# Sampled attention split in two: chosen blocks gathered into DRAM by SyncE, attended after the prompt's attention

## What is computed

```python
def token_mix_sample(xn, cache_cmp, cache_slc, cache_win, wkv, shift, page_table, lw):
    ...
    o_cmp, sel_idx, sel_ok = cmp_attend_select(q, compress(cmp_full, lw), q_pos, slc_full.shape[1] // L_SLC)
    o_slc = slc_attend(q, q_pos, sel_idx, sel_ok, slc_full.reshape(B, -1, L_SLC, 2, N_KV, HEAD_DIM))
    ...
    o_win = window_sample(q, q_pos, win_all, k_pos)
    nsa_out = nsa_combine(gates, o_cmp, o_slc, o_win)

def slc_attend(q, q_pos, sel_idx, sel_ok, kv_blocks):
    ...
    g = kv_blocks[bi, sel_idx, :, :, hi, :]
    s = jnp.einsum('bthgd,bthnld->bthgnl', q, g[..., 0, :]).astype(jnp.float32) * SCALE
    ...
    p = masked_softmax(s, mask[:, :, :, None], axis=(-2, -1))
    return jnp.einsum('bthgnl,bthnld->bthgd', p.astype(g.dtype), g[..., 1, :])
```

## Time and profile before

| | us |
|---|---|
| median of 3 runs | 3992.76 |
| lowest, highest | 3984.46, 3997.12 |
| profiled execution, its own time | 3984.06 |
| its span, first to last instruction | 3982.4 |
| sampled stage, first issue to last store's issue | 1640.09 to 1873.68 |
| prompt's stage, first to last issue of SyncE | 1882.21 to 2203.68 |

### The profile page before, as it was taken

How to read it: one execution, slowest core, us unless ns; L and a number is a source line. 1 busy time by engine, 2 the same in 40 slices (tenths; PEclk the granted TensorE clock), 3 DMA queues, 4 the chain that set the end, 5 groups by cost and what they waited for, 6 DMA issues and landing times. The chain is left out here.

```text
span 3982.4 us, 68983 instructions
## 1 busy us (share of the span) xinstructions
PE 3496.3 (88%) x29788; PEld 3150.0 (79%) x29788; DVE 1489.0 (37%) x1881; ACT 975.6 (24%) x1332; POOL 474.5 (12%) x525
## 2 busy tenths in 40 slices
PE   5999998669927899744799898999999999999998
PEld 5999997358826777522433798999999999999997
DVE  3222220743265767311355323333333333333334
ACT  4111110622213444100243323212212121221112
POOL 1000000444503333200000000000000000000000
PEclk8999997679968999777799999999999999999999
DMA  5343331555515442342300232333333323323332
GB/s 165 108 115 110 93 106 27 192 167 146 119 36 211 179 184 111 98 105 75 109 6 11 80 85 76 95 96 86 96 93 88 96 87 94 96 85 96 91 90 96
DMA packets 501130, 408.07 MB, mean 102 GB/s; under 512 B 142965, under 2 KB 453702, under 8 KB 496262
## 3 DMA queue, kind: packets, MB, share of 16 engines
q1 hardware_dynamic: 454982, 282.91, 25.5%
q0 software_dynamic: 14816, 113.89, 7.8%
q10 hardware_dynamic: 31104, 7.88, 0.9%
HBM read 366.16 MB, written 50.02 MB: 105 GB/s over the span
## 5 line engine op out<-in xcount | busy, mean ns | idle before, releaser
L2574 DVE TENSOR_TENSOR f_w_lo<-wo_raw,f_w_hi 128x2048 fp32r<-128x2048 f32 x132 | 302.5, 2292 | 808.4 <-ACT f_w_hi L2546 808.4
L53 PE MATMUL d_ps<-hh,f_w_hi 128*128 128x260 f32 x2816 | 567.5, 283 | 11.4 <-DVE f_w_lo L2574 11.4
L57 PE MATMUL d_ps<-hh,f_w_lo 128*128 128x260 f32 x2816 | 568.5, 284 | 0.0
L55 PE MATMUL d_ps<-hl,f_w_hi 128*128 128x260 f32 x2816 | 567.6, 283 | 0.0
L2546 ACT CAST f_w_hi<-wo_raw 128x2048 fp32r<-128x2048 f32 x132 | 252.0, 1909 | 995.1 <-DMA wo_raw<-in_w_gate 396.4
L53 PEld LDWEIGHTS d_ps<-hh,f_w_hi 128*128 128x128 f32 x2816 | 435.2, 189 | 11.8 <-DVE f_w_lo L2574 11.8
L57 PEld LDWEIGHTS d_ps<-hh,f_w_lo 128*128 128x128 f32 x2816 | 435.2, 189 | 0.0
L55 PEld LDWEIGHTS d_ps<-hl,f_w_hi 128*128 128x128 f32 x2816 | 433.8, 189 | 0.0
L53 PE MATMUL d_ps<-f_hid_hi,f_w_hi 128*128 128x260 f32 x1408 | 283.7, 283 | 1.2 <-DVE xt L2598 1.2
L57 PE MATMUL d_ps<-f_hid_hi,f_w_lo 128*128 128x260 f32 x1408 | 283.5, 283 | 0.0
L55 PE MATMUL d_ps<-f_hid_lo,f_w_hi 128*128 128x260 f32 x1408 | 282.5, 282 | 0.0
(11 more groups left out here) (431 smaller groups left out, 5941.9 us busy)
## 6 DMA issues: line engine op xcount, KB each, us to landing
p_w<-in_w_in SPq DMA_DIRECT2D x46, 1024.0 KB, 5.6
wo_raw<-in_w_gate SPq DMA_DIRECT2D x44, 1024.0 KB, 5.6
wo_raw<-in_w_up SPq DMA_DIRECT2D x44, 1024.0 KB, 5.6
wo_raw<-in_w_down SPq DMA_DIRECT2D x44, 1024.0 KB, 5.1
wo_raw<-in_w_o SPq DMA_DIRECT2D x16, 1024.0 KB, 6.0
rk_chunks<-r_outb POOLq DMA_DIRECT2D x8, 1280.0 KB, 6.2
s_cur<-rk_chunks SPq DMA_DIRECT2D x8, 1280.0 KB, 7.2
s_one_vecs<-samp_rows SPq DMA_DIRECT2D x80, 128.0 KB, 4.5
```

The costliest lines, as they stand in the source:

```text
L53: pe.matmul(out[j], w_hi, x_hi[j], start=start, stop=False)
L55: pe.matmul(out[j], w_hi, x_lo[j], start=False, stop=False)
L57: last = pe.matmul(out[j], w_lo, x_hi[j], start=False, stop=stop)
L2574: dve.tensor_tensor(w_lo[:, s, :], w_raw[:, s, :], w_hi[:, s, :].bitcast(F32), ALU.subtract).then_inc(lo_done, 1)
```

## The change

The sampled stage becomes two. The first, `stage_nsa_select`, keeps the compressed and the window branch, all of the choice of blocks, and 26 of the gathers. The second, `stage_nsa_picked`, does the attention over chosen blocks, and stands behind the prompt's stage.

- **Gathers.** Their destination is no longer `kbuf` but a new DRAM tensor, `sel_d` [8, 2, 128, 8, 256]. SyncE issues 26 in the first part, 338 in the prompt's stage behind `wo_ahead` (sequences 0, second half, to 6), and ScalarE the 52 of sequence 7 in the second part. The row of addresses is loaded again in each (`places_in`). The page halves that are always attended also go to `sel_d`, all 16 on SyncE.
- **First part.** `win` has 16 slots in memory of its own and GpSimd loads all of them without waiting. ScalarE, not VectorE, copies the turned keys. The importance product moves behind the first turn. The sum of the two branches is kept in `o_part`.
- **Second part.** SyncE loads `sel_d`, keys through three slots and values whole; 16 units, two groups, as before; `o_part` is added; SyncE stores.
- **Prompt.** The four stores move from SyncE to GpSimd, and `mo` has one slot per half instead of two.

```diff
+def gather(eng, g, adr_row, regs, b, heads):
...
+    for hh in heads:
+        for k0 in range(0, 16, 4):
+            at = (b * 4 + hh) * 16 + k0
+            eng.load(regs, adr_row[0:1, at:at + 4])
+            for n in range(4):
...
+                page = eng.snap(regs[n], min_val=0, max_val=places - 1)
+                eng.dma_start(g.sel_d[b, :, lo:lo + C, k // 2, hh * C:(hh + 1) * C].rearrange("v r d -> r v d"),
+                              cache[bass.ds(page, 1), :, :, hh, :].rearrange("a r v d -> r (a v) d")).then_inc(g.sel_kept[b], 16)
...
-                for b in range(NB):
-                    gather(sp, regs, b, 0)
-                sp.wait_ge(os_ready, 1)
...
+                gather(sp, g, adr_row, regs, 0, (0, 1))
...
-                pool.wait_ge(cmp_done, 1)
                 for n in range(2 * NB):
-                    b, kv, s = n % NB, n // NB, n % 3
-                    if 3 <= n < 3 + NB:
-                        pool.wait_ge(kturned, n - 2)
-                    elif n >= 3 + NB:
-                        pool.wait_ge(wv_done, n - 2 - NB)
...
+                for n in range(NB):
+                    act.wait_ge(kturned, n + 1)
+                    if n >= 2:
+                        act.wait_ge(kmm, n - 1)
+                    bank = 2 * (n % 2)
+                    act.copy(kT[:, n % 2, :], ps[:, bank:bank + 2, :].rearrange("p b n -> p (b n)")).then_inc(kept, 1)
...
-                for b in range(2):
-                    gather(act, regs, b, 1)
                 act.wait_ge(nmax_ready, 2)
                 act.activation(sw[:], ps[:, 4, :], ACT.Exp, bias=st[:, 2, 1:2], accum_out=st[:, 2, 2:3]).then_inc(exp_done, 1)
-                for b in range(2, 6):
-                    gather(act, regs, b, 1)
-                picked_exp(0)
...
+def stage_nsa_picked(nc, g):
...
+                def rows_in(dst, b, v, sem_):
+                    sp.dma_start(dst[:, 0:NT - 1, :], g.sel_d[b, v, :, 0:NT - 1, :]).then_inc(sem_, 16)
+                    sp.dma_start(dst[0:C + 1, NT - 1, :], g.sel_d[b, v, 0:C + 1, NT - 1, :]).then_inc(sem_, 16)
+
+                def keys_in(b):
+                    if b >= 3:
+                        sp.wait_ge(kturned, 2 * (b - 2))
+                    sp.wait_ge(g.sel_kept[b], 16 * 4 * (NS - 3))
+                    rows_in(kb[:, b % 3], b, 0, k_in[b % 3])
...
+                keys_in(0)
...
+                            sp.dma_start(qs[a * C:(a + 1) * C, h, :, :], heads[a, :, h]).then_inc(q_in, 16)
+                keys_in(1)
+                keys_in(2)
+                for b in range(NB):
+                    rows_in(vb[:, b], b, 1, v_in[b // 4])
+                    if b + 3 < NB:
+                        keys_in(b + 3)
...
+                    places_in(act, g, adr_row, adr_in)
+                gather(act, g, adr_row, regs, NB - 1, range(4))
...
                 wo_ahead(sp, g)
-                for i in range(4):
-                    sp.wait_ge(o_kept, 4 * i + 4)
-                    sp.dma_start(g.mix_t[D_R + i * 256:D_R + i * 256 + 256, 0:SEQ].rearrange("(g d) t -> d g t", d=C),
-                                 mo[half(i), i // 2, :, :]).then_inc(mix_stored, 16)
-                sp.wait_ge(mix_stored, 16 * 4)
+                regs = [sp.alloc_register(f"picked_place{n}") for n in range(4)]
+                with nc.allow_non_contiguous_dma(reason="small tables"):
+                    places_in(sp, g, adr_row, adr_in)
+                gather(sp, g, adr_row, regs, 0, (2, 3))
+                for b in range(1, NB - 1):
+                    gather(sp, g, adr_row, regs, b, range(4))
...
                 mix_ahead(pool, g)
+                for i in range(4):
+                    pool.wait_ge(o_kept, 4 * i + 4)
...
                 stage_nsa_prompt(nc, g)
+                stage_nsa_picked(nc, g)
```

More of the change, by code:

```diff
@@ L1621, in stage_nsa_sample @@
         adr_ready, adr_out, adr_in = sem("adr_ready"), sem("adr_out"), sem("adr_in")
[L1622 to L1625, removed]
+        win_loaded = [sem(f"win_loaded{n}") for n in range(2 * NB)]
@@ L1631, in stage_nsa_sample @@
-        new = g.kv_rows[SEQ:TC, 512:1024].rearrange("b (v h d) -> b v h d", v=2, h=4)
         pages = g.cache_slc.rearrange("n (t r) w -> n t r w", t=2)
[L1635 to L1656, removed]
@@ L1658, in stage_nsa_sample @@
-        ALL = 16 * 2 * (NS - 3)
+        new = g.kv_rows[SEQ:TC, 512:1024].rearrange("b (v w) -> b v w", v=2)
         with nc.Block() as block:
@@ L1671, in _ @@
                         sp.dma_start(ptb[16 * b:16 * b + 16, :], g.page_table[b:b + 1, :].to_broadcast([16, PG])).then_inc(pt_in, 16)
-                    sp.dma_start(kbuf[C:C + 1, :, NS // 2 - 1].rearrange("p b v h d -> p b (v h d)"),
-                                 g.kv_rows[SEQ:TC, 512:1024].unsqueeze(0)).then_inc(new_in, 16)
-                regs = [sp.alloc_register(f"sp_place{n}") for n in range(4)]
+                    sp.dma_start(g.sel_d[:, :, C, NS // 2 - 1, :], new).then_inc(g.sel_always, 16)
+                regs = [sp.alloc_register(f"sel_place{n}") for n in range(4)]
                 sp.wait_ge(row_in, 32)
-                always(sp, regs, 0)
+                for b in range(NB):
+                    sp.load(regs[0:2], pt_row[0:1, b, :])
+                    for n in range(2):
+                        page = sp.snap(regs[n], min_val=0, max_val=PLACES // 2 - 1)
+                        lo = C - n * C
+                        sp.dma_start(g.sel_d[b, :, lo:lo + C, NS // 2 - 2 + n, :].rearrange("v r w -> r v w"),
+                                     pages[bass.ds(page, 1), n].rearrange("a r (v w) -> r (a v) w", v=2)).then_inc(g.sel_always, 16)
                 with nc.allow_non_contiguous_dma(reason="small tables"):
@@ L1730, in turn @@
                         pe.wait_ge(kept, n - 1)
[L1731 to L1745, removed]
+                    pe.wait_ge(win_loaded[n], 48)
+                    for h in range(2):
+                        for t in range(4):
+                            last = pe.transpose(ps[:, bank + h, t * P:(t + 1) * P], win[:, n, t, h * P:(h + 1) * P], g.ident[:])
                     last.then_inc(kturned, 1)
@@ L1749, in mult @@
                     pe.wait_ge(kept, n + 1)
[L1750 to L1762, removed]
+                    for h in range(2):
+                        last = pe.matmul(ps[:, 4, :], query(n, h, 0, P), kT[:, n % 2, h * 512:(h + 1) * 512],
+                                         start=(n + h == 0), stop=(n + h == NB))
                     last.then_inc(kmm, 1)
@@ L2060, in _ @@
                 mix_ahead(pool, g)
+                for i in range(4):
+                    pool.wait_ge(o_kept, 4 * i + 4)
+                    pool.dma_start(g.mix_t[D_R + i * 256:D_R + i * 256 + 256, 0:SEQ].rearrange("(g d) t -> d g t", d=C),
+                                 mo[half(i), :, :]).then_inc(mix_stored[i % 2], 16)
+                for s in range(2):
+                    pool.wait_ge(mix_stored[s], 32)
             @block.tensor
@@ L2204, in keep_out @@
                     act.wait_ge(pv_done, first_block[2 * m + 1] + t + 1)
-                    act.copy(mo[half(i), i // 2, :, t * P:(t + 1) * P],
+                    if i >= 2 and t == 0:
+                        act.wait_ge(mix_stored[i % 2], 16)
+                    act.copy(mo[half(i), :, t * P:(t + 1) * P],
                              ps[half(i), 6 + m % 2, :].rearrange("p (q t) -> p q t", q=4)).then_inc(o_kept, 1)
@@ L2848, in build @@
     g.adr_d = nc.dram_tensor("adr_d", [P, 16], I32, kind="Internal").ap()
+    g.sel_d = nc.dram_tensor("sel_d", [NB, 2, P, 8, 256], F32, kind="Internal").ap()
+    g.sel_always = nc.alloc_semaphore("sel_always")
+    g.sel_kept = [nc.alloc_semaphore(f"sel_kept{b}") for b in range(NB)]
     g.mix_t = nc.dram_tensor("mix_t", [D, TC], F32, kind="Internal").ap()
@@ L2860, in build @@
         retire_sems(nc, g)
+        g.o_part, g.gts, g.own = (ctx.enter_context(nc.sbuf_tensor(n, [P, w], F32)) for n, w in (("o_part", C), ("gts", 3), ("own", 8)))
         nsa(nc, g)
```

275 lines of the change are left out of this document (185 added, 90 removed).

## The result

The changed kernel takes **3960.4 us** (median of 5 runs, 3951.2 to 3965.3) against 3992.8 for the kernel before. The ratio of the two is 0.9918, with a 95% interval from 0.9899 to 0.9938: faster by 0.8%. Timed again beside other kernels (4 runs) it gave 0.9906 [0.9890, 0.9923]. The forecast was 4010, slower; it had the wrong sign, though the time lies in its range, which reached down to the rival without a surcharge.

What follows compares the result with a forecast made beforehand. The gather was taken to be limited by an engine's issue time per copy, not by transfers. Terms -174 + 98.6 + 92.6 = +17 us on the profiled 3984.1, 8.7 below the median of 3992.8, gave 4010; range 3942 to 4060.

Steps and rivals of the forecast that it cites:

- Step 1: First part of the sampled stage: gets shorter, ending at 1702 against 1876.2, -174 us.
- Step 2: Prompt's stage: lasts until SyncE issues its last of 338 gathers; +43.6 us at the old pace, +98.6 at 1.01.
- the formula: Prompt's stage: last gather issued at 1965.2 + 338 x, x us per gather, against the old end at 2207.95.
- Step 3: Gather's issue into DRAM: 0.70 us instead of 0.537, so 1.01 us per gather instead of 0.847.
- Fetched anew each time: Rival on the gather's issue: 0.957 us, so 1.27 per gather; +117 us, 4110; chance 0.07.
- hidden: Rival: under 0.718 us per gather, the prompt's stage keeps its length; -91 us, 3902; chance 0.05.
- no surcharge: Rival on the gather's issue: stays 0.537 us into DRAM, 0.847 per gather; -46 us, 3946; chance 0.30.
- Step 4: New second part behind the prompt's stage: 83.4 us plus 9.2 waiting for the last sequence's late keys, +92.6 us.
- break-even of 0.966: Whole kernel: time per gather at which gain turns to loss, an issue of 0.66 us.

Runs made afterwards that it cites:

- e1: Changed kernel without the 104 gathers of sequences 1 and 2 in the prompt's stage; whole 3901.2 us, prompt's stage 327.7.
- e5: Changed kernel with the last sequence's 52 gathers and the address table's load on GpSimd in the prompt's stage; 3940.8 us, ratio to before 0.9881.
- e4: Kernel before with all 416 gathers on SyncE and none on ScalarE, destination still the core's own memory; 4163.7 us.
- e3: Changed kernel with all 416 gathers in the first part, half on SyncE and half on ScalarE, none later; 4053.7 us.
- e7: Changed kernel repeated unaltered beside other kernels; 3955.0 us.
- e6: Changed kernel with 208 gathers on GpSimd and 182 on SyncE in the prompt's stage, none on ScalarE in the second part; 3899.4 us, ratio to before 0.9775.

## Why the prediction was wrong

**Step 1 (-174) held: -177.8.** ScalarE copies the keys in 1.01 us, inside its slack, and GpSimd's loads are never late. From start to end of work it is -176.1; the other 1.7 lie in the seam behind, 4.3 us instead of 6.0. Two things inside it were off. The values took less, and the arithmetic ends 58.6 us after the stage's start instead of 61.9:

```profile
1689.08 11.50 PE L1720 MATMUL b_ps<-b_win,b_pTw 128*32 128x256 f32 x64 [0.78 <-DVE b_pTw L1846]
```

That is 11.5 against 8 x 1.91 = 15.3. And the address write, which took 1.1 us before, waited 9.5 us (waits of SyncE's queue):

```profile
SPq L1668 <- DMA adr_d<-b_adr: 9.5, 1, 9.5
```

So SyncE's 26 gathers end at 1703.8, 1.4 us behind VectorE, where they were to be 4 ahead. In this stretch the windows' loads, now issued without waiting, fill the DMA engines:

```profile
1660.00:1683.00 23.00, 22.59 (x105) 14.15 (x104) 6.72 (x34) 8.66 (x10) 15.92 (x27) 1.00 0.93 311
```

In all nine profiles with this first part the write waits 7.6 to 11.1 us. That the loads hold it back is argued from their coincidence and was not tested.

**Step 2 (the stage ends with SyncE's last issue) held as a mechanism**, which e1 shows. Its start was off: the gathers begin 88.5 us into the stage, not at 83.0, mostly since the table's issue and landing behind three loads of 1 MB took 8 us and not 3.6. e5, where GpSimd loads the table ahead, has the start at 81.4. With x as measured, the formula gives 1965.2 + 338 x 0.867 - 2208.0 = +50.3, and with the 5.5 it gives +55.8, against the +56.0 that was measured.

**Step 3 failed, and the sign of the forecast with it.** The term that was mis-sized is the issue of one gather. I had put 0.70 us for an issue whose destination is DRAM, from copies of rows between DRAM tensors (0.613 to 0.639) plus a difference in shape. The measured value is 0.534. The one row that pointed there, 0.538 among the window copies, was also the row that I set aside; and those copies differ from the gather in much else. e4 and the changed kernel put both destinations beside each other: 0.537 and 0.534. The pace is then 0.867 and not 1.01, worth 338 x 0.143 = 48 us in the prompt's stage alone. "Fetched anew each time" and "hidden" are out as well: the median is the minimum, and no issue is shorter. The argument for "fetched anew" misread its row, too: 0.957 is the 21st gather of SyncE, at 1686.3, and the first took 0.587. The rival "no surcharge" was the right case. Its 3946 is 14 us below the median, but that it comes so near is partly luck: its sum was -46 and the stages gave -22.7.

The pace itself is not a constant: 0.811 in the first part, 0.848 in e4, 0.859 to 0.872 for the 338 gathers of the prompt's stage in four profiles. Over 338 gathers the step from 0.811 to 0.867 is 19 us. Nine of the 338 issues are longer than 0.6 us, up to 1.9, which adds 7.5 us; the gaps between issues are also longer (0.310 on average against 0.285). What lengthens either is open.

**Step 4 (+92.6) had the wrong wait.** With x = 0.867 it would have given 83.4 and 1.8 for late keys, 85.2. It measured 99.1 and 93.6. The bare length was right (83.0 in e3, 82.9 in e5). What I missed is the order of ScalarE's program: 52 issues stand ahead of the first exponential, which was wanted 33.6 us into the stage and came at 55.0. The wait, and the slower values behind it, are all of the excess over the bare 83.0: 14.45 + 2.28 = 16.7 for 16.1 in the first profile, 8.59 + 2.03 = 10.6 for 10.6 in e7. I had read this very pattern in the kernel before and counted it as removed, and did not look where the new stage has its own.

**The sum by what was measured**: -177.8 for -174, +56.0 for +98.6, +99.1 for +92.6. Of the error of 40 us in this sum, 43 are the prompt's stage, which is the surcharge (48) less the late table (5.5); the rest nearly cancels (-3.8 and +6.5). The median is 50 us below the forecast and not 40: the profiled run stood 4.3 above its median where that of before stood 8.7 below (13), less 3 by which the other stages ran longer. The measured paces, 0.867 and 0.944 (49.06 / 52), lie below the break-even of 0.966 that the prediction named, and the sign followed.

## What to carry over

When a transfer is bound by its issue, count it as instructions of the engine that issues: ask how many fit beside the other work of that stage, and give the rest to another free engine, not to the one whose next arithmetic others wait for. Work moved under cover is hidden only as far as the cover reaches; here some 63 of 338 gathers stuck out and gave back 55 of 178 us. And price an operation whose one operand changes by the same operation's own row, unless a row of the same shape speaks against it.

## What the hardware showed

- The issue of a gather of 64 rows on SyncE costs the same into DRAM (0.534) and into the core's own memory (0.537).
- GpSimd gathers faster than SyncE: 0.70 to 0.72 us a gather (52 in 36.4, 208 in 150.6 us) against 0.81 to 0.90, though its issue is longer. Its rows stand back to back four at a time with 0.35 between, about the 0.32 that reading four addresses takes; so the arithmetic on each address is off its path.
- GpSimd's drain at the end of the prompt's stage is 0.8 us in the changed kernel without gathers, 5.1 with 52, and 8.9 to 9.2 with 208, even 80 us after the last of them (e6). The next stage begins only behind it. Gathers are not all that counts: in the kernel before, where GpSimd's program ended right behind its loads of `mix_raw` and `xt`, the same stage's drain is 21.9 us (it starts at 1885.5, so it is hidden), and behind the 48 window loads of the new first part it is 15.4. The Trainium skill, page "VectorE: DVE Perf Modes", section "The DRAIN you can't avoid", knows drains of about 12 ns each on all five engines, from the code ahead of and behind a kernel; SyncE's at the ends of the stages here are 7 to 380 ns, and GpSimd's are the long ones above.
- A small write to DRAM waited 9.5 us while loads kept the DMA engines 0.93 busy at 311 GB/s, and 1.1 us in the kernel before, where they were 0.42 busy at 62 GB/s in those 2 us. That the load is the cause was not tested.
